# Dot-row tokens copied to two PSUM banks during the latent and context units, with the recurrence's products moved into the other banks

## The reference, cut to what matters

```python
# mixer, one of its two branches: a recurrence over tokens, 16 heads of 64, forwards and backwards
S = S * w_t - (S @ kk_t) (kk_t * a_t)^T + v_t k_t^T ;  y_t = S @ r_t
# PEER: for each token 8 heads x 16 chosen experts = 128 rows of two tables of 16384 x 1024
u = jnp.take(p['peer_u'], eidx, axis=0)                      # 128 rows of 4 KB for each token
act = gelu(einsum('td,thkd->thk', hc, u)) * gw               # 128 dot products for each token
v = jnp.take(p['peer_v'], eidx, axis=0)
out = einsum('thk,thkd->td', act, v)                         # 128 rows, weighted and summed
```

## Time and profile before

| | |
|---|---|
| median of 3 runs | 4824.75 us (4816.26, 4824.75, 4826.09) |
| the profiled execution's own time | 4815.76 us |
| its span, first to last instruction | 4814.0 us |
| granted TensorE clock, mean | 0.868 of full speed |
| busy: PE, DVE, ACT, POOL | 73%, 52%, 21%, 36% |
| HBM read | 1113 MB |
| latent units of layer 0 | 1133 to 1620 us |
| context units of layer 1 | 1998 to 2465 us |

### The profile page before, as it was taken

One profiled execution on the slowest core, in us unless ns is written; L12 is line 12 of the kernel. 1 busy time (PEld: TensorE's weight loads), 2 busy tenths in 40 slices (PEclk: granted clock), 3 DMA queues, 4 the chain that ended last, 5 costly groups with the idle time before them and its releaser, 6 DMA issues. The chain is left out here.

```text
span 4814.0 us, 86196 instructions
## 1 busy us (share of the span) xinstructions
PE 3492.9 (73%) x35566; PEld 2677.7 (56%) x35566; DVE 2497.2 (52%) x5810; ACT 1017.3 (21%) x2594; POOL 1749.7 (36%) x1745
## 2 busy tenths in 40 slices
PE   7989986896777796767645799997430315788798
PEld 6877765785555564655421587776400001676687
DVE  2846637767776337977640044663869260343410
ACT  1234421132222211332210123442100000212200
POOL 0000000445887345778877200000577777000000
PEclk9999998898888897878878899998765758899999
DMA  5423224997999687889999542003699999312342
GB/s 215 140 90 132 116 97 150 338 350 262 344 353 339 255 330 293 328 293 338 348 373 409 197 145 71 3 3 111 252 397 405 408 408 408 107 69 87 111 177 79
DMA packets 299480, 1122.89 MB, mean 233 GB/s; under 512 B 33744, under 2 KB 39136, under 8 KB 289760
## 3 DMA queue, kind: packets, MB, share of 16 engines
q0 software_dynamic: 221184, 805.40, 44.6%
q1 hardware_dynamic: 77920, 312.15, 17.7%
HBM read 1113.22 MB, written 4.19 MB: 232 GB/s over the span
## 5 line engine op out<-in xcount | busy, mean ns | idle before, releaser
L2183 POOL DMA_INDIRECT ring<-in_peer_u,expert_number x399 | 464.3, 1164 | 796.9 <-DVE expert_number L2521 566.5
L2166 PE MATMUL psum<-spare,picked 128*32 128x512 f32 x1392 | 243.6, 836 | 461.3 <-POOL picked L2217 363.6
L2140 DVE CUSTOM_DVE_ANT_0 ring<-ring,tok 128x1024 f32<-128x1024 f32 x399 | 482.6, 1225 | 120.3 <-DMA ring<-in_peer_u,expert_number 104.4
L2166 PEld LDWEIGHTS psum<-spare,picked 128*32 128x32 f32 x1392 | 53.2, 136 | 639.7 <-issue 639.7
L2197 POOL DMA_INDIRECT spare<-in_peer_v,expert_turned x348 | 333.0, 957 | 94.8 <-issue 87.6
L186 PE MATMUL psum<-h,weight_ring 128*128 128x256 f32 x1472 | 329.0, 388 | 22.6 <-PEq L98 22.6
L186 PEld LDWEIGHTS psum<-h,weight_ring 128*128 128x128 f32 x1472 | 287.2, 196 | 63.8 <-issue 23.9
L1859 PE MATMUL psum<-h,weight_ring 128*128 128x256 f32 x1344 | 294.3, 381 | 3.2 <-PEq L98 3.2
L1859 PEld LDWEIGHTS psum<-h,weight_ring 128*128 128x128 f32 x1344 | 255.4, 191 | 40.8 <-issue 7.2
L1348 PE MATMUL psum<-h,weight_ring 128*128 128x256 f32 x1056 | 237.2, 387 | 8.7 <-PEq L98 8.7
L1348 PEld LDWEIGHTS psum<-h,weight_ring 128*128 128x128 f32 x1056 | 204.0, 194 | 40.9 <-issue 12.7
(11 more groups left out here) (628 smaller groups left out, 7614.4 us busy)
## 6 DMA issues: line engine op xcount, KB each, us to landing
weight_ring<-in_w_in SPq DMA_DIRECT2D x210, 512.0 KB, 3.6
ring<-in_ada_w SPq DMA_DIRECT2D x24, 1024.0 KB, 11.6
weight_ring<-in_w_q SPq DMA_DIRECT2D x48, 512.0 KB, 3.5
weight_ring<-in_ada_w SPq DMA_DIRECT2D x16, 1024.0 KB, 6.4
weight_ring<-in_w_out SPq DMA_DIRECT2D x32, 512.0 KB, 3.5
gate_ring<-in_w_gate SPq DMA_DIRECT2D x32, 512.0 KB, 3.4
weight_ring<-in_w_mlp_in SPq DMA_DIRECT2D x32, 512.0 KB, 3.4
ring<-in_w_mlp_out SPq DMA_DIRECT2D x8, 2048.0 KB, 7.9
```

The source lines that it names most:

```text
L2140: dve.tensor_tensor_reduce(place.rows, place.rows, b.tok[:, tile, :], 1.0, 0.0, ALU.mult, ALU.add, b.dots[:, tile, slot:slot + 1]).then_in ...
L2166: mm = pe.matmul(out, place.window.columns[:, strip, first:first + STRIP], part.rows[:, 512 * half:512 * half + 512], start=(m % BATCHES = ...
L2183: pool.indirect_dma_start(place.rows, None, b.tables["u"], bass.IndirectOffsetOnAxis(ap=b.number[:, r:r + 1], axis=0)).then_inc(place.sem, 16)
```

## The change

`hold_tokens` is a new small stage: ACT copies the 1024 values for each partition of one token tile from SBUF (`tok`) to PSUM banks 2 and 3. It runs ahead of a unit when the job's next dot row is in a tile that is not held yet: ahead of the first latent unit (tile 0), ahead of the second (tile 1), ahead of the first context unit (tile 0) and ahead of the fourth (tile 1). `use_rows` then takes the tokens from PSUM for rows of the held tile; the other input and the output stay in SBUF.

Banks 2 and 3 are therefore not free for the units, and the units' products move:

- V is turned into bank 5 instead of 2, so PE waits for ACT's copies of V (L902) already ahead of the pair products.
- The next unit's low-rank products are in the halves of banks 0 and 1.
- R and state products are in banks 0 and 1, U in the right halves of banks 4 and 5, Y as before in the left halves.
- Context units: the Gram products of i = 0 and i = 1 share banks 0 and 1 (256 columns each); their order doesn't change.
- Latent units: the Gram products of i = 0 fill banks 0 and 1. Those of i = 1 are made later, in the same banks, by PE after step 5 of the inversion, once DVE has masked the first ones (a new wait of PE on DVE). DVE masks them after step 7 (a new wait of DVE on PE), where it did so after step 5.

All other units (layer 0's context mixer, layer 1's latent mixer) run without a job and keep their banks and order.

```diff
+            unit.second_gram(q, pe)
             if q == 8 and unit.following is not None:
-                pe.wait_ge(k.vec_step.sem, unit.marks["G"])
+                pe.wait_ge(k.vec_step.sem, unit.marks["G", 1])
                 unit.following.low_rank(pe)
...
+    wide = emit and k.tokens_at is None
+    in_turn = emit and not wide
+    turned_bank = k.bank(2 if wide else 5)
+    def gram(i, hh):
+        if in_turn:
+            return k.bank(hh)
+        return k.bank(2 * i + hh) if wide else k.bank(hh)[:, 256 * i:256 * i + 256]
+    def of_r(i):
+        return k.bank(2 * i if wide else i)
+    def of_u(i):
+        return k.bank(2 * i + 1) if wide else k.bank(4 + i)[:, 256:512]
...
             pe.wait_ge(k.vec_step.sem, marks["kt"])
+            if sweep == 0 and not wide:
+                pe.wait_ge(k.act_step.sem, marks["V"])
...
+            mm = multiply_gram(pe, 0)
+            if not in_turn:
+                mm = multiply_gram(pe, 1)
...
+            second = 7 if in_turn else 5
+            if q == 7 and in_turn:
+                dve.wait_ge(k.second_grams.sem, k.second_grams.at(1))
-            if q in (4, 5):
-                i = q - 4
+            if q in (4, second):
+                i = int(q == second)
...
+        def second_gram(q, pe):
+            if q == 5 and in_turn:
+                pe.wait_ge(k.vec_step.sem, marks["G", 0])
+                multiply_gram(pe, 1).then_inc(k.second_grams.up(), 1)
...
+                expert_turn(k)
+                if (unread or spills) and k.tokens_at != k.job.row // SLOTS and k.job.row < 2 * SLOTS:
+                    hold_tokens(k, k.job, k.job.row // SLOTS)
                 rwkv_unit(k, u, operands, units[n + 1] if n + 1 < len(units) else None, mod, n)
...
-        dve.tensor_tensor_reduce(place.rows, place.rows, b.tok[:, tile, :], 1.0, 0.0, ALU.mult, ALU.add, b.dots[:, tile, slot:slot + 1]
+        tokens = k.psum[:, 1024:2048] if k.tokens_at == tile else b.tok[:, tile, :]
+        dve.tensor_tensor_reduce(place.rows, place.rows, tokens, 1.0, 0.0, ALU.mult, ALU.add, b.dots[:, tile, slot:slot + 1]
...
+def hold_tokens(k, job, tile):
+    with k.stage() as block:
+        @block.scalar
+        def _(act):
+            for half in range(2):
+                part = slice(512 * half, 512 * half + 512)
+                act.activation(k.bank(2 + half), job.shared.tok[:, tile, part], ACT.Copy).then_inc(k.act_step.up(), 1)
+    k.tokens_at = tile
```

More of the change, by code:

```diff
@@ L763, in product @@
         k = self.k
-        return k.bank(i)[:, 256 * which:256 * which + 256] if self.first else k.bank(2 * i + which, 256)
+        return k.bank(i)[:, 256 * which:256 * which + 256] if self.first or not self.emit or k.tokens_at is not None else k.bank(2 * i + which, 256)
     def low_rank(self, pe, counted=True):
@@ L879, in rwkv_unit, with multiply_gram @@
     cols = 128 if emit else 64
+    def multiply_gram(pe, i):
+        for n in range(2):
+            for j in range(2):
+                c, at = 2 * i + n, (2 * n + j) * cols
+                for hh in range(2):
+                    h = half(hh)
+                    rhs = KR[h, 0:2, j, 64 * c:64 * c + 64] if emit else KR[h, 0, j, 64 * c:64 * c + 64]
+                    out = gram(i, hh)[:, at:at + cols]
+                    if emit:
+                        out = out.rearrange("p (a t) -> p a t", a=2)
+                    mm = pe.matmul(out, b.C[h, j, c].rearrange("p s t -> p (s t)"), rhs, start=True, stop=True)
+        return mm
     marks = {}
@@ L901, in _ @@
                 for hh in range(2):
-                    act.activation(b.W[half(1 - hh), :, :, hh, :], k.bank(2)[half(1 - hh)].rearrange("p (c j v) -> p c j v", c=4, j=2), ACT.Copy
+                    act.activation(b.W[half(1 - hh), :, :, hh, :], turned_bank[half(1 - hh)].rearrange("p (c j v) -> p c j v", c=4, j=2), ACT.Copy
                                    ).then_inc(k.act_step.up(), 1)
@@ L1063, in _ @@
                         h = half(hh)
-                        ins = act.activation(W[h, chunk(i, n), :, hh, :], k.bank(2 * i + 1)[h, 0:P].rearrange("p (j v) -> p j v", j=2), ACT.Copy)
+                        ins = act.activation(W[h, chunk(i, n), :, hh, :], of_u(i)[h, 0:P].rearrange("p (j v) -> p j v", j=2), ACT.Copy)
                     ins.then_inc(k.act_step.up(), 1)
@@ L1072, in _ @@
                         out = b.S[:, i, j] if n == 0 else states[i][:, j]
-                        ins = act.activation(out, k.bank(2 * i)[:, 64 * j:64 * j + 64], ACT.Copy, scale=operands.pc[:, j, c:c + 1])
+                        ins = act.activation(out, of_r(i)[:, 64 * j:64 * j + 64], ACT.Copy, scale=operands.pc[:, j, c:c + 1])
                     ins.then_inc(k.act_step.up(), 1)
@@ L1159, in _ @@
                             h, at = half(hh), 64 * j
-                            mm = pe.matmul(k.bank(2 * i)[h, at:at + 64], b.CT[:, c, j, h], W[:, c, j, hh, :], start=not summed, stop=True,
+                            mm = pe.matmul(of_r(i)[h, at:at + 64], b.CT[:, c, j, h], W[:, c, j, hh, :], start=not summed, stop=True,
                                            skip_group_check=True)
@@ L1437, in rwkv @@
                 k.job.shared.slots, k.job.away = own, False
+        k.tokens_at = None
         if not emit:
```

23 lines of the change are left out of this document (12 added, 11 removed).

## The result

The changed kernel takes 4737.24 us (median of 4 runs, 4732.00 to 4747.48) against 4821.76 for the kernel before (4 runs, 4816.26 to 4826.09): a ratio of 0.983, interval 0.981 to 0.985. It is faster by 84 us where the prediction had 59; the time lies inside its range (4735 to 4803), 2 us above the lower edge. The profiled execution took 4732.0 us, with a span of 4730.2 against 4814.0, so that traces differ by 83.8 us, as the times do.

A forecast was written before the change was run, and what follows sets the result against it. POOL was taken to bound ten units, DVE the four with dot rows alone. Terms -67 - 2 + 0 + 7.6 + 2.4 + 0 gave -59 us; forecast 4763 us, range 4735 to 4803 for 8 in 10.

The forecast's parts named there:

- The bound and the cause: Ten units with both kinds of gather: POOL is the bound, its gathers held up by dot rows with two SBUF inputs.
- The size of the delay: Ten units: 135 gathers held up by dot rows take 89.2 us over 0.937 us each; all 427 gathers' excess is 94.
- How much of it would come through: Ten units: between 45 and 89 us of the delay gained, middle taken, -67 us.
- Seventh latent unit: Nine dot rows there delayed five gathers by 4.3 us; half of that gained, -2 us.
- Dot rows alone: Four units with dot rows but not both kinds of gather: DVE sets them, no change, 0; upper side 4 us.
- Four hold stages: Stages that copy tokens to PSUM: 1.9 us each, four times, +7.6 us; upper bound 12.
- V ahead of the pair products: Eight units of sweep 0: PE waits 0.3 us for ACT's copies of V, +2.4 us, at most 4.
- Gram products of i = 1 later: Latent units, products moved behind step 5: 0, with 1.8 us remaining before DVE needs step 8; bounds -1 to +1 per unit.
- Buffers or DMA taking over: Rival: under half of the 89 us comes through, net -10 to -35 us, 4785 to 4810; chance 0.18.
- More than all of it: Rival: units with dot rows alone gain too, from shorter rows and earlier data; net beyond -80, under 4740; chance 0.04.
- That it doesn't do what it is for: Rival: the accumulating instruction holds the port for another reason than its second SBUF input; only +10 remain, 4834; chance 0.05.
- PE's new wait: Rival: latent units, PE's wait for first masks delays step 8; at 10 us each +11 net, 4836; chance 0.02.

The follow-up runs named there:

- half of the bytes: Changed kernel with `peer_u` gathers in stages with held tokens fetching 2 KB for each partition instead of 4 KB: 4736.4 us, 0.982 of the kernel before.
- the extra stages: Changed kernel with a hold stage ahead of every unit with a job, sixteen in place of four: 4746.75 us, 0.985 of the kernel before.
- the copies inside the unit: Changed kernel with ACT's two copies at the head of the unit's own program, without hold stages: 4731.3 us (0.981), again 4729.94 us (0.980).
- the jobless units with the same order: Changed kernel with the new bank layout also in the 16 units that host no gathers: 4736.18 us, 0.983 of the kernel before.

## Why the prediction was right, and where it was off

**The bound and the cause: right.** POOL's issue was the bound of ten units, and the second SBUF input of the dot row was what made it slow. The run with rows from SBUF shows the second by itself; half of the bytes shows that the first is POOL's issue and not the transfers, but for 6 to 9 us. One reading of the prediction was off: that POOL waits for no buffer in the kernel before. It waited there 2.0 us at 1202.47 and 3.8 at 2162.68 for PE to free one.

**The size of the delay: right for the dot rows.** They make 89.2 us. The check beside it was off: the 427 gathers count four twice, at borders of stretches; it is 423, with an excess of 99.1 in place of 94, so that DVE's other instructions had some 10 us and not 5. After the change 13.9 are left, 85 gone. What is left is nearly all (13.0) in gathers beside DVE's other instructions with two SBUF inputs, such as the one at 1251.40, which met a product of `KR`:

```profile
1251.23 0.69 DVE L948 TENSOR_TENSOR KR<-kk,E 128x512 f32<-128x512 f32 x1 [0.40 <-PEq L99]
1251.40 1.33 POOL L2239 DMA_INDIRECT weight_ring<-in_peer_v,expert_turned  x1 [0.30 <-SPq L99]
1251.84 0.68 DVE L952 TENSOR_TENSOR KR<-z,E 128x512 f32<-128x512 f32 x1
```

**How much of it would come through: the term that was mis-sized.** The prediction took 67 of 89 us, three quarters, the middle of its bounds of 45 and 89, because buffers and a nearly full DMA queue might give back the remainder. Measured are 81.0 us of units for 81.5 us of gathers. Term by term: POOL's idle time in the ten units did grow, from 647.9 - 516.5 = 131.4 us to 566.9 - 427.7 = 139.2, by 7.8; in the order of time its gaps over 0.45 us, which are waits and not issue, add up to 18.0 us in place of 10.1, which is all of it, and 3 of these 8 us are the end of the last unit, where POOL is through with its work. But its weight copies, which the prediction didn't count, got shorter by 7.3 us, from 21.02 in these units to 13.69: dot rows held them up too. The kernel before, POOL's and the copies' sums over the ten units (the first line is of all engines) and one copy in order of time:

```profile
sum 647.90, PE 436.24 PEld 314.12 DVE 431.39 ACT 175.93 POOL 516.51; mean PE 43.62 PEld 31.41 DVE 43.14 ACT 17.59 POOL 51.65
...
sum 647.90, POOL 21.02; mean POOL 2.10
...
1272.12 1.22 DVE L2140 CUSTOM_DVE_ANT_0 g<-g,tok 128x1024 f32<-128x1024 f32 x1
1272.35 1.03 POOL L2214 COPY picked<-weights 128x4 f32<-128x4 f32 x1
```

Such a copy takes 0.20 us in the median after the change; this one takes 1.03 and ends 0.04 us behind the dot row. The two, +7.8 and -7.3, nearly cancel, and the gathers' 81.5 us are left whole. The fear of the DMA ceiling was mostly unfounded: the queues do run at 404 to 410 GB/s in most of these units, as high as anywhere, but taking a quarter of the bytes away shortened the ten units by 6 to 9 us only, and gave nothing that the total can tell.

**Seventh latent unit: -2 forecast, -3.9 in the traces** (65.5 to 61.6); other traces of the changed kernel have 60.4 and 59.5, so the half taken was too little there.

**Dot rows alone: 0, right.** Rows of 1215 ns in place of 1225 gave nothing: the first two context units went from 47.1 and 46.4 us to 46.9 and 46.3. The Trainium skill's extra cycles for PSUM (VectorE: DVE Perf Modes, § "The TRN2 errata") don't show: by them a row would have been 65 ns longer, and it was 10 shorter.

**Four hold stages: +7.6 forecast.** One adds 1.46 us to DVE's path, not 1.9. The stage itself takes what was added up: 0.38 in, 1.12 for the two copies and 0.36 out are 1.86 us. What the sum left out is that a plain boundary costs DVE 0.40 us in any case. Where DVE sets the length the price is whole (1.5 us by the extra stages); where POOL does it is near 0.2 by one trace, not to be told from nothing. None of the four lies between two units that POOL sets. Two of them are at the end of a unit that can be compared: the third context unit is 1.3 us longer than before, and the first latent unit, at 54.9, is 1.0 longer than with the copies inside the unit (54.0 and 53.9). With 1.46 for the other two, the four are some 5 us.

**V ahead of the pair products: +2.4 forecast.** The wait is there, 0.38 us and up to 0.4, but only three of seven units showed one (1.1 us together), and the jobless units with the same order were no longer.

**Gram products of i = 1 later: 0, right.** PE's wait for the first masks was 5.1 us over five units, and 1.57 us remained ahead of step 8 where 1.8 were forecast.

**Sum.** By the traces: ten units -81.0, seventh latent unit -3.9, third context unit with its stage +1.3, the first latent and the first two context units -0.5 together: -84.1, where the spans differ by 83.8. Against the forecast of -59 that is 25 us more: 14 from the share (81 for 67), 2 from the seventh unit, and 9 from the small costs, forecast at 10 and seen at 0.8 in these units. Two hold stages lie ahead of the first units and so outside this sum; the unchanged stages ahead of the latent units took from 1131 to 1142 us in the traces, which is spread enough to hide 3 us.

**The rivals.** Buffers or DMA taking over: POOL's idle time came (+7.8 us), in the size of a tenth of the gain and not of half. More than all of it through shorter rows (net beyond -80, under 4740): by its number this is where the run landed, below the forecast's own 4740 to 4793, and it had a chance of 0.04; but its mechanism is not it, as the dot-rows-alone units gained 0.5 us in all. The mechanism was the forecast's, with a larger share come through. That it doesn't do what it is for: excluded. PE's new wait: it exists (0.49 us in the unit shown, 2.9 at the longest), and PE still ends step 8 before DVE takes it up there.

## What to carry to other kernels

An engine that is busy a third of the span can be the bound of the stages that matter; to find out whether it rests there, add its gaps between instructions to its busy time and compare with the stage's length; after the change POOL has the least busy time of PE, DVE and POOL in the latent unit shown, and still sets it. When a small instruction of one engine has two durations, list what another engine runs at those times: here the end of the long ones stood at a fixed distance behind the end of another's instruction. Where POOL and DVE run side by side, an operand that DVE reads again and again is better in PSUM, and all of the rows that meet POOL must be moved: moving every second one brought a quarter of the gain here, because only about every second one of a run had held up a gather.

## What the runs showed of the hardware

A gather that a DVE instruction with two SBUF inputs holds up ends 0.81 us behind that instruction's end; undisturbed it takes 0.94, so all but its first 0.13 us come behind the hold. A gather that begins before the dot row is hardly held: the 71 that began in the 0.2 us ahead of one in the kernel before took 0.99 us at most. A POOL copy that begins inside such a row ends with it (0.04 to 0.05 us behind). The Trainium skill (SBUF — State Buffer, § "Who interferes with whom") calls DVE's second port pair, shared with GpSimd, an exclusive lock; these traces agree, with 1.98 us in place of 0.94, and show it for the issue of an indirect DMA as well, where the same section's inferred remark has `tensor_tensor` leave descriptor generation alone: the gather of 1.33 us beside a `TENSOR_TENSOR` of two SBUF inputs, above, says otherwise. By the same instruction with its tokens in PSUM none of 282 gathers was delayed (0.97 us at most). The pace of indirect gathers of 128 rows hardly depends on their size: 0.94 + 0.30 us with rows of 4 KB, 0.95 + 0.30 with 2 KB.
